# The two attention mixers of the first block: where weight splits, squares, a Silu and score maxima stand in the engines' queues

## The reference, cut to what matters

```python
# first block, each layer: x += 0.5 * swiglu(norm(x)); x += mixer(norm(x)); x += 0.5 * swiglu(norm(x))
...
def mla_gla_mixer(...):            # layer 0
    c_q, c_kv, k_r, g_q, g_k, g_v, g_a, g_r = split_cols(u @ w_in, HY_SPLITS)
    o_mla = mla_heads(...)         # 8 heads, causal softmax over keys of 64 + 32 columns
    o_gla = gla_heads(...)         # 4 heads, chunked linear attention, then rms_norm and a silu gate
    return concatenate([o_mla, o_gla]) @ w_out
...
def nsa_mixer(...):                # layer 1
    q, k_c, v_c, k_s, v_s, k_w, v_w, g = split_cols(u @ w_in, NSA_SPLITS)
    ...                            # compressed keys: silu(flat @ w1) @ w2, softmax over 15 blocks
    return (gb[0] * o_c + gb[1] * o_s + gb[2] * o_w) @ w_out    # 16 heads, gated
```

## Time and profile before

| | |
|---|---|
| median of 3 runs | 1707.72 us (1703.98 to 1708.02) |
| profiled execution | 1702.22 us |
| its span | 1700.4 us |
| TensorE busy | 1646.4 us, 97% of the span |
| VectorE busy | 1149.6 us, 68% |
| ScalarE busy | 915.8 us, 54% |
| granted TensorE clock, mean | 0.989 |

### The profile page before, as it was taken

One profiled execution on the slowest core, in us unless ns is written; L12 is line 12 of the kernel. 1 busy time (PEld: TensorE's weight loads), 2 busy tenths in 40 slices (PEclk: granted clock), 3 DMA queues, 4 the chain that ended last, 5 costly groups with the idle time before them and its releaser, 6 DMA issues.

```text
span 1700.4 us, 25492 instructions
## 1 busy us (share of the span) xinstructions
PE 1646.4 (97%) x9631; PEld 1402.3 (82%) x9631; DVE 1149.6 (68%) x1628; ACT 915.8 (54%) x1468; POOL 115.4 (7%) x130
## 2 busy tenths in 40 slices
PE   7999998999999999998999999899999999999998
PEld 6888896888888888987688888887888898788887
DVE  5766655566657666678856666776867677677765
ACT  5444566454455444535754445665655566655553
POOL 0000011000001000131000000310000020110000
PEclk9999998999999999999999999999999999999999
DMA  7555452265555555532035554622555553245552
GB/s 267 197 190 193 155 184 87 110 237 180 190 175 192 180 195 181 181 134 100 2 142 193 193 178 172 174 83 100 183 200 179 196 169 129 82 161 181 179 198 90
DMA packets 42221, 276.76 MB, mean 163 GB/s; under 512 B 7057, under 2 KB 7970, under 8 KB 9250
## 3 DMA queue, kind: packets, MB, share of 16 engines
q1 hardware_dynamic: 40434, 271.00, 45.8%
q0 software_dynamic: 1712, 4.73, 1.4%
HBM read 274.66 MB, written 1.05 MB: 162 GB/s over the span
## 4 chain that ended last, share of the span: by engine, by line
PE 86%; DVE 7%; ACT 4%; DMA 1%; issue 1%; POOL 0%; SPq 0%; DVEq 0%; ACTq 0%; POOLq 0%
PE bank L782 29%; PE bank L800 22%; PE bank L783 14%; PE bank L726 3%; DVE w_lo L1870 2%; PE bank L932 2%; PE bank L685 1%; PE bank L933 1%; PE bank L934 1%; PE bank L686 1%; PE bank L687 1%; DMA raw<-in_stream 1%; DVE prob L2244 1%; PE bank L1048 1%; PE bank L984 1%
## 5 line engine op out<-in xcount | busy, mean ns | idle before, releaser
L782 PE MATMUL bank<-xt_both,w_hi 128*128 128x512 f32 x2112 | 746.6, 398 | 5.6 <-DVE xt_both L1907 5.2
L1870 DVE TENSOR_TENSOR w_lo<-raw,w_hi 128x2048 fp32r<-128x2048 f32 (+1 forms) x254 | 580.4, 2285 | 182.3 <-ACT w_hi L1405 181.6
L783 PE MATMUL bank<-xt_both,w_lo 128*128 128x256 f32 x2112 | 590.1, 279 | 0.0
L1405 ACT ACTIVATE w_hi<-raw 128x2048 fp32r<-128x2048 f32 (+1 forms) x254 | 484.8, 1910 | 80.9 <-PE bank L687 53.1
L782 PEld LDWEIGHTS bank<-xt_both,w_hi 128*128 128x128 f32 x2112 | 397.4, 188 | 104.5 <-DVE w_lo L1896 3.5
L783 PEld LDWEIGHTS bank<-xt_both,w_lo 128*128 128x128 f32 x2112 | 398.9, 189 | 2.3
L1625 ACT ACTIVATE KT<-bank 128x256 f32<-128x256 f32 x264 | 86.9, 381 | 338.6 <-PE bank L783 338.6
L800 PE MATMUL bank<-w_hi,h_lo 128*128 128x512 f32 x528 | 208.2, 394 | 0.0
L800 PE MATMUL bank<-w_hi,h_hi 128*128 128x512 f32 x528 | 208.2, 394 | 0.0
L800 PE MATMUL bank<-w_lo,h_hi 128*128 128x512 f32 x528 | 208.2, 394 | 0.0
L800 PEld LDWEIGHTS bank<-w_hi,h_hi 128*128 128x128 f32 x528 | 99.5, 188 | 23.6 <-issue 0.5
(11 more groups left out here) (344 smaller groups left out, 2043.1 us busy)
## 6 DMA issues: line engine op xcount, KB each, us to landing
raw<-in_stream SPq DMA_DIRECT2D x255, 1024.0 KB, 4.9
work<-in_rpb POOLq DMA_DIRECT2D x32, 64.0 KB, 6.6
X<-in_x SPq DMA_DIRECT2D x2, 512.0 KB, 5.0
prob<-in_cmp_w POOLq DMA_DIRECT2D x1, 1024.0 KB, 7.0
O<-in_cmp_w POOLq DMA_DIRECT2D x1, 1024.0 KB, 12.8
out<-X SPq DMA_DIRECT2D x1, 1024.0 KB, 4.0
cst<-in_consts SPq DMA_DIRECT2D x1, 712.0 KB, 10.4
O<-in_final_gain POOLq DMA_DIRECT2D x1, 512.0 KB, 5.8
```

The costliest lines, as they stand in the source:

```text
L782: pe.matmul(both, w_hi[:, sl, cols], xt_both[:, :, k, :], start=(k == 0), stop=False)
L783: ins = pe.matmul(dst[:, 0:S], w_lo[:, sl, cols], xt_hi[:, k, :], start=False, stop=(k == KD - 1))
L1405: act.activation(to, src, ACT.Copy).then_inc(hi_done, 1)
L1870: dve.tensor_tensor(to, src, hi.bitcast(F32), ALU.subtract).then_inc(lo_done, 1)
```

## The change

It reorders instructions in the two mixers of the first block. No instruction is added and none is removed.

- **Scores two duos ahead.** TensorE issues `scores(0)`, `scores(1)`, and then `scores(m + 2)` ahead of `turn_p(m)`; VectorE does `maxima` of duos 0 and 1 first, and then those of duo m + 2 right after `scale` of duo m, ahead of the aside work.
- **Splits into the tails.** The splits of `mix0`'s units 1 and 2 leave the start of the first attention. ScalarE splits unit 1 ahead of the squares and unit 2 in the last turn of the loop; VectorE splits them in the last two turns. In the second mixer the same holds for VectorE's splits of `mix1`'s units 1 and 2 and for ScalarE's of unit 2; VectorE's split of `mix1`'s unit 0 goes behind the compressed scores.
- **Squares around evictions.** ScalarE does four squares, its two evictions of query groups, then the other four squares; VectorE does its two evictions ahead of the mean of the squares.
- **Silu ahead of a split.** In block 5 of the second mixer ScalarE does the Silu ahead of the split of unit 8 and of the eviction of block 5.
- **Smaller moves.** VectorE's compressed scores go behind its rotation of block 8, its last key eviction goes from block 10 to block 9, and TensorE waits for `c_kcT` only between its first two and its next two groups of transposes.

```diff
@@ TensorE, attention
                 scores(0)
+                scores(1)
                 for m in range(n_duos(stage)):
-                    scores(m + 1)
+                    scores(m + 2)
@@ TensorE, nsa_step, c == 7
-                    pe.wait_ge(c_kcT, 1)
                     pe.wait_ge(ft_ready_d, 2)
                     pe.wait_ge(ft_ready_p, 2)
-                    feature_major("nsa", 0, 4)
+                    feature_major("nsa", 0, 2)
+                    pe.wait_ge(c_kcT, 1)
+                    feature_major("nsa", 2, 4)
@@ ScalarE, project
-                    split(u0 + c + NSPLIT)
+                    if u0 + c + NSPLIT < U["mix1"] + 2:
+                        split(u0 + c + NSPLIT)
@@ ScalarE, attention, end of a turn
                     pair_out(stage, pair_done(stage, m - 2))
+                    if m == n_duos(stage) - 1:
+                        split(U[{"mla": "mix0", "nsa": "mix1"}[stage]] + 2)
@@ ScalarE, the Silu of c == 5: from nsa_step (after) to nsa_before (before)
@@ ScalarE, ahead of the first attention
-            split(U["hy_in"] + 7 + NSPLIT)
-            act.wait_ge(g_o, 1)
-            for t in range(NT):
+            def out_squares(t):
                 for h in range(GLA_H):
...
+            split(U["mix0"])
+            split(U["mix0"] + 1)
+            act.wait_ge(g_o, 1)
+            out_squares(0)
             feature_major("mla", 1)
-            split(U["uq"] + NSPLIT)
+            out_squares(1)
@@ ScalarE, gla_out_hi
-                split(U["ukv"] + NSPLIT)
@@ VectorE, project
-                    split(u0 + c + NSPLIT)
+                    if u0 + c + NSPLIT < U["mix1"]:
+                        split(u0 + c + NSPLIT)
@@ VectorE, attention
                 if early:
                     early()
+                maxima(2)
+                maxima(3)
                 for m in range(n_duos(stage)):
                     scale(2 * m)
                     scale(2 * m + 1)
+                    maxima(2 * m + 4)
+                    maxima(2 * m + 5)
                     if aside and m == 0:
                         aside()
-                    maxima(2 * m + 2)
-                    maxima(2 * m + 3)
                     lo_part(pair_done(stage, m - 2))
+                    if m >= n_duos(stage) - 2:
+                        split(U[{"mla": "mix0", "nsa": "mix1"}[stage]] + m - n_duos(stage) + 3)
@@ VectorE, nsa_step
-                if c == 8:
-                    compressed_scores()
                 if c == 9:
                     compressed_probabilities()
+                    feature_major("nsa", 4)
                 if c == 10:
-                    feature_major("nsa", 4)
@@ VectorE, nsa_rotate, behind the rotation
+                if c == 8:
+                    compressed_scores()
+                    split(U["mix1"])
@@ VectorE, ahead of the first attention
-            split(U["hy_in"] + 7 + NSPLIT)
+            split(U["mix0"])
+            feature_major("mla", 1)
             dve.wait_ge(g_sq, 8)
             mean_squares(16, 8, 1.0 / GLA_DV).then_inc(g_ms, 1)
-            feature_major("mla", 1)
```

More of the change, by code:

```diff
@@ L1753, in nsa_step @@
             def nsa_step(c):
-                if c == 5:
-                    for m, b in enumerate((4, 5)):
-                        act.wait_ge(c_b, m + 1)
-                        dst = hid[m].rearrange("p (g n) -> p g n", g=4)[:, :, 0:NCMP]
-                        src = bank[b][:, 0:60].rearrange("p (g n) -> p g n", g=4)
-                        act.activation(dst, src, ACT.Silu, bias=small[:, 0, m:m + 1]).then_inc(c_hid, 1)
                 if c == 7:
@@ L1769, in nsa_step, with nsa_before @@
                     feature_major("nsa", 4)
-            def nsa_exp(c):
+            def nsa_before(c):
+                if c == 5:
+                    for m, b in enumerate((4, 5)):
+                        act.wait_ge(c_b, m + 1)
+                        dst = hid[m].rearrange("p (g n) -> p g n", g=4)[:, :, 0:NCMP]
+                        src = bank[b][:, 0:60].rearrange("p (g n) -> p g n", g=4)
+                        act.activation(dst, src, ACT.Silu, bias=small[:, 0, m:m + 1]).then_inc(c_hid, 1)
                 if c == 9:
@@ L1839, in _ @@
             norm(4)
-            project("nsa", U["nsa_in"], NSA_BLOCKS, nsa_step, nsa_exp)
+            project("nsa", U["nsa_in"], NSA_BLOCKS, nsa_step, nsa_before)
             attention("nsa")
```

## The result

The kernel before took 1705.79 us and the changed one 1695.36 us (medians of five runs each on one chip; 1703.32 to 1708.02 and 1688.23 to 1696.28). The ratio is 0.993, with a 95% interval of 0.9906 to 0.9953. The profiled execution took 1693.07 us, with a span of 1691.3 us, against 1702.22 and 1700.4 before: 9.15 less.

A forecast was written before the change was run, and what follows sets the result against it. TensorE, busy 97% of the span, was taken as the bound, leaving its waits and lower clock; 7.9 + 0.4 + 3.8 - 1.5 + 3.7 = 14.3 us, taken as 14.0, made 1707.72 into 1693.7, range 1688 to 1702.

The forecast's parts named there:

- The rival of the low clock: Lower clock through the first attention and again at the second's start: gain 7 to 10 us, some 1699; chance 0.25.
- a loop that keeps 3.19: Second attention: another wait or latency replaces the removed one, 3.19 us a duo stays; gain 10.3, 1697.4 us; chance 0.12.
- a second attention at the lower clock: Second attention at half clock, about 5 us a duo: slower kernel, 1724 us if all 16 duos; chance 0.05.
- First mixer, start: First attention: scores start at about 275.4 instead of 277.44, 2.0 us earlier; the squares end at 276.9, not 275.8.
- First mixer, size: First attention: gain between 2.4 and 9.2 us, taken as 7.9 with one short fall of the clock.
- the chain of 9.2: First attention: VectorE's chain puts the last duo's transposes at 293.7 instead of 302.90, 9.2 us earlier before clock losses.
- the term for a fall until 291: First attention: a lower clock until 291 us costs 3.6 us; until 284 it costs 1.4, until 298 6.8.
- Block 5: Second mixer: Silu's 2.99 us wait moves to block 7 as 5.6; gain 0.4, clock's fall behind it costs 1.5.
- It restarts at 763.0 instead of 763.39: Second mixer, block 7: TensorE's restart after waiting for VectorE's rotation, a gain of 0.4 us.
- Blocks 8 to 10: Second mixer: VectorE's chain of 17.9 or 18.0 us brings first transposes 3.8 us sooner, or 2.4 after the clock's fall.
- The loop: Second attention: TensorE becomes the bound at 3.0 us a duo instead of 3.19; gain 3.7 us, ends 1.8 and 4.0.
- Splits in the tails: Ends of both attentions: moved splits hidden under TensorE's twelve products (2.86 us), later weight loads hidden with some 8 us spare.

The follow-up runs named there:

- the two sets: The changed kernel as it is, timed twice against the kernel before: 1695.36 us first, 1691.79 us when timed again beside follow-up kernels.
- two ahead alone: Kernel before with scores and maxima two duos ahead and nothing else: 1703.04 us, first mixer 122.07, second 168.77.
- the rotation ahead of the splits: Changed kernel with VectorE rotating blocks 4 and 5 ahead of the splits of its blocks 5 and 6: 1687.47 us, second mixer 160.15.
- the three edits together: Changed kernel with first attention one duo ahead, VectorE's rotation before splits in blocks 5 and 6, and ScalarE's wait on its eighth square dropped: 1683.15 us median.

## Why the prediction was right, and where its terms were off

The forecast was 1693.7 us with 14.0 us less than before. The changed kernel took 1695.36 and 1691.79 in the two sets, 10.4 and 13.7 less than the kernel before beside it. That the first time lies only 1.7 from the forecast is in part luck: the kernel before came out at 1705.79, 1.9 below the 1707.72 that the forecast started from, and the gain is 3.6 short. What differs between the sets is the clock. Over the eleven timed executions of the changed kernel, the three with a mean granted clock of 0.993 or 0.994 took 1686.93 to 1689.78 us, and the eight with 0.987 to 0.991 took 1690.11 to 1696.28. In the profiles it fell in the first attention of the first set's and not in that of the second set's. The rival of the low clock has that half right (it gave the first mixer 2.4 to 5.6, and 5.3 was measured). Its other half, a fall at the start of the second attention, isn't in the rows: the clock is 1.00 from 788 to 806 us. The rivals of a loop that keeps 3.19 and of a second attention at the lower clock are ruled out by the loop's rows. Step by step:

- **First mixer, start: right.** The first scores were put at 275.4, which is 67.0 us behind the norm's root (208.41); they came at 66.9. The squares were put at 68.5 and ended at 68.3.
- **First mixer, size: 7.9 forecast, 5.3 and 8.5 measured.** The bounds were 2.4 to 9.2. At full clock the chain gave 8.5 (124.07 less 115.61), or 9.4 without the wait ahead of the table (124.07 less 114.72), so the chain of 9.2 was right to 1 us, and what it missed is the load of the table. (One short fall off 9.2 is 7.8 by the prediction's own numbers, not 7.9.) The rest is the clock: the same program took 3.2 us more when its granted clock was 0.67 to 0.80 at 280 to 291. That is the term for a fall until 291 (3.6), where I had taken that for one until 284 (1.4).
- **Block 5: +0.4 forecast, -0.9 measured.** That the Silu's 2.99 us were worth nothing was right, and so was the new wait, but for its size (5.6 forecast, 1.53 and 5.04 found). The step that failed is "It restarts at 763.0 instead of 763.39". It took the rotation's steps at the length that they had. GpSimd's half came 4.8 us earlier, behind an earlier TensorE, and collided with them: 1.3 us. The fall of the clock behind the gap, 1.5 forecast, is 1.7 in the transposes' row (3.67 less 1.97). So the Silu's move is no gain but a loss: 1.8 us by undoing it in the changed kernel, and 3.0 by making it alone.
- **Blocks 8 to 10: 2.4 forecast with the fall, 0.7 measured.** VectorE's chain from the start of the rotation to the first maxima was forecast at 17.9 or 18.0 and took 18.1 (771.85 to 789.96). Its start was off: it came at 68.5 us behind the norm's root, where the 773.6 of the working is 65.3, and 66.8 with the fall. The difference is the late restart of block 7 (1.3) and 0.4 that no run places. The sum of the prediction calls its 3.8 for these blocks "with the fall counted already"; it is the value without the fall (2.4 is with it), so taking 1.5 off beside it was right and the words are not.
- **The loop: 3.7 forecast, 4.9 measured.** TensorE became the bound, as forecast, but a duo takes it 2.88 and not 3.0. My 2.98 to 3.07 came from a mean in which the second duo still held the tail of a wait; without any wait the two duos take 3.06 and 2.70. In 20 us of the loop TensorE is busy for all 20, VectorE 19.4.
- **Splits in the tails: right.** They cost nothing where they went. In the 30 us from the last transposes on, TensorE is busy for 29.52 in the changed kernel (838 to 868) and for 29.52 before (848.5 to 878.5), so the splits and the later loads stayed hidden. The wait of 0.72 in the last turn but one is not theirs: it is there, at 0.73 and 0.72, with the splits in their old places and with two ahead alone.

The second mixer as a whole: 6.1 forecast, 5.55 measured, by two errors that nearly cancel (its first transposes 1.7 later than forecast, its loop 1.2 shorter).

What stays open is why the clock falls in one execution of the first attention and not in another. Rows with the same busy time in front of them go either way. The squares around the evictions and the smaller moves were not run alone: that the first scores come 2.1 us sooner (66.9 us behind the norm's root, against 69.0 before and with two ahead alone) is shown for them together. It also wasn't tried to take the exponentials' latency out of the first attention's third scores in another way than by the table.

## What to carry to other kernels

A wait that is taken from an engine makes all that depends on the engine earlier, also on engines that nobody looked at: ask which two of them now work at the same time and slow each other, as VectorE's steps of 0.29 became 0.50 here. Where a transfer of work "is worth nothing", look at what stands ahead of the step that really ends last, as two splits of weights for later blocks did here; that was worth 4.7 us, more than the scores two duos ahead (3.8). And before a difference of a few microseconds in a short stretch is given to an edit, profile the unedited kernel twice, and see where the difference begins: what is there ahead of the first edited instruction is not the edit's (1.7 us with two ahead alone).

## What the runs showed of the hardware that was not expected

- The table of the exponential is loaded behind the wait for the first maxima (278.29, after 1.02 idle) if another wait of the same engine stands between the last square and it, and right behind the square (276.95) if not. The load takes 1.28 us each time.
- The granted clock of one and the same program was 0.67 to 0.80 at 280 to 291 us in one execution and 1.00 in another, with TensorE busy for 2.36 of 4 us at 284 to 288 in the one with the fall and 2.19 of 4 in the one without. The page "TensorE: Matmul & The Clock Gate" of the Trainium skill (section "Why this matters for your kernels") says that a gap between bursts of matmuls puts the clock back to half rate. In block 7 of the second mixer the trace agrees wherever the gap is 5.04 or 5.43 us: the clock is at 0.50 behind it in all eight profiles that have such a gap.
- Behind shorter gaps the clock went either way. Behind 2.99 in block 5 it was 0.56 in the kernel before and 1.00 with two ahead alone. Behind 0.53 and 1.62 in block 7 it fell to 0.50 with the rotation ahead of the splits, and not with the three edits together. In the first attention it went either way behind 2.17 and 2.16, and behind 1.81. And in one execution, that with the Silu back, it fell at 269 us with no gap in front: TensorE had been busy for all of the 7 us before and stayed so.

```profile
262.00:269.00 7.00, 7.00 (x42) 5.61 (x40) 2.87 (x4) 6.80 (x10) 0.00 (x0) 1.00 0.02 4
269.00:273.00 4.00, 4.00 (x15) 3.03 (x14) 2.29 (x1) 1.90 (x2) 0.00 (x0) 0.53 0.20 31
```

- VectorE's step of 128 by 128 with two inputs takes 0.50 beside GpSimd's and 0.29 without, in every one of the four kernels looked at.
